# Differential attention woven into reordered key, value and query slots, its bias rows made in the glu slots, and its norm sums by plain fp32 matmuls

## The reference, cut to what matters

```python
def shared_kv(x, kv_norm, kv_w, k_norm):
    kv = rms_norm(x, kv_norm) @ kv_w
    nk = 2 * N_HEADS * HEAD_DIM
    k = rms_norm(kv[..., :nk].reshape(bsz, seqlen, N_HEADS, 2, HEAD_DIM), k_norm)
    v = kv[..., nk:].reshape(bsz, seqlen, N_HEADS, 2 * HEAD_DIM)
...
def diff_attention(h, k, v, rel_bias, w_q, q_norm, ...):
    q = rms_norm((h @ w_q).reshape(bsz, seqlen, N_HEADS, 2, HEAD_DIM), q_norm)
    ...
        bias = rel_bias[t5_causal_bucket(rel)].astype(f32).transpose(2, 0, 1)
        s = jnp.einsum("bqhcd,bkhcd->bhcqk", qc, k).astype(f32) * scale
        s = s + bias[None, :, None]
        s = jnp.where(rel <= 0, s, NEG_INF)
        pm = jax.nn.softmax(s, axis=-1)
        attn = pm[:, :, 0] - lam * pm[:, :, 1]
        return jnp.einsum("bhqk,bkhe->bqhe", attn.astype(v.dtype), v)
    ...
    o = rms_norm(o, subln) * (1.0 - lam_init)
    return o.reshape(bsz, seqlen, N_HEADS * 2 * HEAD_DIM) @ w_o
```

## Time and profile before

| What | Value |
|---|---|
| Median of 3 runs | 1396.17 us (1394.51 to 1400.16) |
| The profiled execution | 1395.5 us |
| Its span, first to last instruction | 1393.6 us |
| PE busy in the span | 1321.2 us (95%) |
| POOL, ACT, DVE busy | 1017.5, 687.4, 683.8 us |
| Mean granted PE clock | 0.974 |

### The profile page before, as it was taken

How to read it: one execution, slowest core, us unless ns; L and a number is a source line. 1 busy time by engine, 2 the same in 40 slices (tenths; PEclk the granted TensorE clock), 3 DMA queues, 4 the chain that set the end, 5 groups by cost and what they waited for, 6 DMA issues and landing times.

```text
span 1393.6 us, 27925 instructions
## 1 busy us (share of the span) xinstructions
PE 1321.2 (95%) x11024; PEld 1265.1 (91%) x11024; DVE 683.8 (49%) x1175; ACT 687.4 (49%) x960; POOL 1017.5 (73%) x794
## 2 busy tenths in 40 slices
PE   6989999999999689999999959999999999999999
PEld 6879999999989469999998837999999998899999
DVE  8994555556545866555565694211113454311112
ACT  7716544444656676444456445544445444644442
POOL 1227988888778418888878672888887765888885
PEclk9999999999999799999999968999999999999999
DMA  6314555555456305555554430555554432455540
GB/s 256 122 62 152 189 182 182 181 181 181 152 138 244 121 1 190 182 181 181 181 181 152 153 121 31 182 182 181 181 181 164 177 118 95 152 182 182 182 149 30
DMA packets 33879, 217.07 MB, mean 156 GB/s; under 512 B 3683, under 2 KB 7428, under 8 KB 8196
## 3 DMA queue, kind: packets, MB, share of 16 engines
q1 hardware_dynamic: 30096, 211.14, 42.9%
q10 hardware_dynamic: 3700, 4.75, 1.4%
HBM read 213.26 MB, written 2.62 MB: 155 GB/s over the span
## 4 chain that ended last, share of the span: by engine, by line
PE 78%; DVE 12%; ACT 5%; issue 3%; POOL 1%; DMA 1%; DVEq 0%; ACTq 0%; SPq 0%; POOLq 0%
PE up L1349 18%; PE up L1350 17%; PE up L1351 17%; PE acc L1349 6%; PE acc L1351 6%; PE acc L1350 6%; ACT w_hi L417 2%; PE up L1469 1%; DVE opnd L795 1%; DVE mix L1117 1%; DVE mix L1235 1%; DVE mix L804 1%; DVE s_work L935 1%; DVE mix L1132 1%; DVE mix L1131 1%
## 5 line engine op out<-in xcount | busy, mean ns | idle before, releaser
L340 POOL TENSOR_TENSOR w_lo<-ring,w_hi 128x512 fp32r<-128x512 f32 x764 | 985.0, 1322 | 291.8 <-ACT w_hi L417 282.0
L1349 PE MATMUL up<-opnd,w_hi 128*128 128x256 f32 x2208 | 631.8, 286 | 8.7 <-POOL w_lo L340 2.2
L1350 PE MATMUL up<-opnd,w_lo 128*128 128x256 f32 x2208 | 625.3, 283 | 0.0
L1351 PE MATMUL up<-opnd,w_hi 128*128 128x256 f32 x2208 | 625.2, 283 | 0.0
L417 ACT ACTIVATE w_hi<-ring 128x2048 fp32r<-128x2048 f32 x193 | 368.3, 1910 | 267.5 <-PE up L1351 213.8
L1349 PEld LDWEIGHTS up<-opnd,w_hi 128*128 128x128 f32 x2208 | 424.0, 192 | 19.8 <-issue 10.9
L1350 PEld LDWEIGHTS up<-opnd,w_lo 128*128 128x128 f32 x2208 | 424.2, 192 | 0.4
L1351 PEld LDWEIGHTS up<-opnd,w_hi 128*128 128x128 f32 x2208 | 424.1, 192 | 0.0
L1349 PE MATMUL acc<-opnd,w_hi 128*128 128x256 f32 x736 | 208.5, 283 | 2.5 <-DVE opnd L1033 2.5
L1350 PE MATMUL acc<-opnd,w_lo 128*128 128x256 f32 x736 | 208.3, 283 | 0.0
L1351 PE MATMUL acc<-opnd,w_hi 128*128 128x256 f32 x736 | 208.3, 283 | 0.0
(11 more groups left out here) (238 smaller groups left out, 1358.9 us busy)
## 6 DMA issues: line engine op xcount, KB each, us to landing
ring<-in_stream SPq DMA_DIRECT2D x197, 1024.0 KB, 4.8
bias_rows<-mix ACTq DMA_DIRECT2D x1, 1536.0 KB
mix<-in_s_b SPq DMA_DIRECT2D x1, 1024.0 KB, 6.5
x<-in_x SPq DMA_DIRECT2D x1, 1024.0 KB, 8.5
mix<-in_s_c SPq DMA_DIRECT2D x1, 1024.0 KB, 12.5
mix<-bias_rows ACTq DMA_DIRECT2D x1, 1024.0 KB, 5.1
out_x<-x SPq DMA_DIRECT2D x8, 128.0 KB, 1.7
mix<-in_p ACTq DMA_DIRECT2D x2, 256.0 KB, 3.4
```

Of the source, the lines that this page charges most:

```text
L340: ins = nc.gpsimd.tensor_tensor(w_lo[:, b, cols], ring[:, r, cols], w_hi[:, b, cols].bitcast(f32), ALU.subtract)
L1349: MM(o, l_hi, r_hi, start=start, stop=False, skip_group_check=True)
L1350: MM(o, l_lo, r_hi, start=False, stop=False, skip_group_check=True)
L1351: return MM(o, l_hi, r_lo, start=False, stop=stop, skip_group_check=True)
```

## The change

- The 12 slots of `kvq` are taken in the order q0 q1 k0 v0 k1 q2 k2 v1 q3 k3 v2 v3, and the queries' operand is made before the keys'. SP's list of slots is written out for this stage.
- Attention runs between half-slots: `DIFF_AT` says after which half the scores of a head run, `DIFF_PV` the same for its values, `DIFF_OUT` for its output. The first two slots of `wo` are spread over the last half-slots by a table, as for the stick stage.
- Both query blocks of a head are one step now: four score matmuls, three transposes into one bank, one ACT copy, and values with 256 and 128 columns.
- Squares of the head norms are summed by one plain fp32 matmul of 512 columns; the rounded copy, DVE's remainder and `d_half_r` are gone.
- The one-hot load, the bias matmul and its copy move to glu slots 1, 4 and 5. ACT issues the 1.5 MB write right after the last glu slot, and the read back before ple0.

```diff
-UNITS = ["s5", "ffn0", "ple0", "kv", "q", "diff", "ffn1", "ple1", "even", "mixed", "ffn2",
+UNITS = ["s5", "ffn0", "ple0", "q", "kv", "diff", "ffn1", "ple1", "even", "mixed", "ffn2",
...
+DIFF_ORDER = ["q0", "q1", "k0", "v0", "k1", "q2", "k2", "v1", "q3", "k3", "v2", "v3"]
+DIFF_AT = [8, 10, 12, 14, 16, 18, 22, 24]
+DIFF_PV = [12, 14, 16, 18, 22, 23, 26, 28]
+DIFF_OUT = [19, 20, 20, 21, 25, 26, 29, 31]
+DIFF_HALVES = 32
...
@@ scalar engine, glu loop and after it
+                if m == 1:
+                    act.dma_start(d_oh, a["bias_oh"]).then_inc(dma["bias_oh"], 16)
...
+            c.wait("bias_sb")
+            act.dma_start(a["scratch"], d_row.unsqueeze(1).broadcast_to([HEADS, P, 384])).then_inc(dma["bias_w"], 16)
...
             act.dma_start(f_pe[:, 0:2], a["p0"]).then_inc(dma["pe0"], 16)
             pe_operand(0)
             ffn(0, "ple0")
-            ple(0, ["kv", "q"])
+            act.wait_ge(dma["bias_w"], 16)
+            act.dma_start(d_bias, a["scratch_toeplitz"]).then_inc(dma["bias_r"], 16)
+            ple(0, ["q", "kv"])
...
@@ vector engine, glu loop
+                if m == 5:
+                    c.wait("bias_ps")
+                    c.up_and_wait(V.tensor_copy(d_row, aux[0][0:HEADS, 0:384]), "bias_sb")
...
@@ tensor engine
+                if m == 4:
+                    pe.wait_ge(dma["bias_oh"], 16)
+                    c.up(MM(aux[0][0:HEADS, 0:384], d_oh[:, 384:384 + HEADS], d_oh[:, 0:384], start=True, stop=True),
+                         "bias_ps")
...
+            def diff_stats(n):
+                c.wait("hn_sq")
+                ...
+                c.up(MM(acc[:, 3], d_half, d_sq[:, n % 2], start=True, stop=True, skip_group_check=True), "hn_ssq")
...
+            fill = {24: [(0, range(4))], 25: [(1, range(4))], 26: [(0, [4]), (1, [4])], 27: [(0, [5]), (1, [5])],
+                    30: [(0, [6]), (1, [6])], 31: [(0, [7]), (1, [7])]}
+            for t in range(DIFF_HALVES):
+                i, half = t // 2, t % 2
+                if i < 12:
+                    if half == 0:
+                        o = begin_slot(S + i)
+                    diff_half(i, half, o)
+                for h in heads_at(DIFF_AT, t):
+                    diff_scores(h)
+                for g, ks in fill.get(t, []):
+                    if ks[0] == 0:
+                        banks[g] = begin_slot(wo + g)
+                    slot_part("diff", wo + g, banks[g], ks, fresh=(g == 0))
+                for h in heads_at(DIFF_PV, t):
+                    diff_values(h)
+                for h in heads_at(DIFF_PV, t - 1):
                     c.wait("o_sq")
                     c.up(MM(aux[h % 2][:, T:2 * T], ones, d_q[:, h], start=True, stop=True), "o_ssq")
+                for n in stats_at(t):
+                    diff_stats(n)
+                for h in heads_at(DIFF_AT, t - 2):
+                    diff_transposes(h)
```

More of the change, by code:

```diff
@@ L315, in listed @@
                     load(s % RING, slice(streamed(s), streamed(s) + 1))
[L317 to L321, removed]
+            done = RING
+            for name in ("kvq", "qkv"):
+                first = START[name] // RING * RING
+                steady(done, (first - done) // RING)
+                done = first + 3 * RING
+                listed(first, done)
+            steady(done, (N_SLOTS - done) // RING)
             listed(N_SLOTS // RING * RING, N_SLOTS)
@@ L688, in _, with diff_square, diff_root @@
[L688 to L692, removed]
+            def diff_square(n):
+                if n >= 2:
+                    act.wait_ge(sem("qk_ready"), n - 1)
+                c.wait("hn_raw")
+                c.up(A(d_sq[:, n % 2], d_tmp[:, n % 3], ACT.Square), "hn_sq")
+            def diff_root(n):
+                c.wait("hn_ssq")
+                b = d_sq[:, n % 2]
+                c.up_and_wait(A(b, acc[:, 3], ACT.Ln, scale=1.0 / HD, bias=eps), "hn_ln")
+                c.up(A(b, b, ACT.Exp, scale=-0.5), "hn_rstd")
@@ L1141, in _ @@
             ffn(0, "ple0")
-            ple(0, ["kv", "q"])
+            ple(0, ["q", "kv"])
             S, u0 = START["kvq"], BANK["kvq"]
[L1146 to L1152, removed]
-            c.wait("rstd")
+            c.wait("rstd")
@@ L1155, in diff_normed, with diff_projection @@
+            def diff_projection(i):
+                kind, g, u = DIFF_ORDER[i][0], int(DIFF_ORDER[i][1]), (u0 + i) % 2
+                if kind == "v":
+                    if g == 0:
+                        c.wait("rstd_tok")
+                    values(S + i, u, d_v[:, :, g * 256:(g + 1) * 256], 256)
+                    c.tell("up_free")
+                    c.tell("diff_v")
+                else:
+                    head_raw(DIFF_NORMED.index(i), S + i, u, d_tmp)
             def diff_normed(n):
+                name = DIFF_ORDER[DIFF_NORMED[n]]
+                g = int(name[1])
@@ L1161, in diff_normed, with diff_logits @@
                                                      ALU.mult, ALU.mult), "qk_ready")
[L1163 to L1181, removed]
+            def diff_logits(h):
+                c.wait("diff_scores")
+                for qb in range(2):
+                    nk = P * (qb + 1)
+                    L = d_l[:, qb].rearrange("p (c k) -> p c k", c=2)[:, :, 0:nk]
+                    bias = d_bias[:, h, 0:T] if qb else d_bias[:, h, P:T]
+                    c.up_and_wait(V.scalar_tensor_tensor(L, acc[:, 0:2, P * qb:P * qb + nk], HD ** -0.5,
+                                                         bias.unsqueeze(1).broadcast_to([P, 2, nk]), ALU.mult, ALU.add),
+                                  "diff_read")
+                    c.up(V.tensor_reduce(d_st[:, 40 + 2 * qb:42 + 2 * qb], L, AX.X, ALU.max, negate=True), "diff_max")
@@ new lines, in diff_probs @@
+            def diff_probs(h):
+                if h:
+                    c.wait("diff_at_ps")
+                for qb in range(2):
+                    nk = P * (qb + 1)
+                    L = d_l[:, qb].rearrange("p (c k) -> p c k", c=2)[:, :, 0:nk]
+                    c.wait("diff_exps", 2)
+                    r = d_st[:, 48 + 2 * qb:50 + 2 * qb]
+                    step(V.reciprocal(r, d_st[:, 44 + 2 * qb:46 + 2 * qb]))
+                    step(V.tensor_scalar(L[:, 1], L[:, 1], r[:, 1:2], neg_lam, ALU.mult, ALU.mult))
+                    c.up(V.scalar_tensor_tensor(d_a[:, qb, 0:nk], L[:, 0], r[:, 0:1], L[:, 1], ALU.mult, ALU.add),
+                         "diff_probs")
+                dve.wait_ge(sem("diff_probs"), c.of("diff_probs").value())
@@ new lines, in _ @@
+            for t in range(2, DIFF_HALVES):
+                if t % 2 == 0 and t <= 24:
+                    diff_projection(t // 2 - 1)
+                for n in stats_at(t - 2):
+                    diff_normed(n)
+                for h in heads_at(DIFF_AT, t - 1):
+                    if h == 0:
+                        dve.wait_ge(dma["bias_r"], 16)
+                    diff_logits(h)
+                for h in heads_at(DIFF_AT, t - 2):
+                    diff_probs(h)
+                for h in heads_at(DIFF_PV, t - 3):
@@ L1663, in _ @@
             assert used[0] == BANK["kvq"]
[L1664 to L1692, removed]
+            def diff_half(i, half, o):
+                b, kind = (S + i) % SPLIT, DIFF_ORDER[i][0]
+                name = "q" if kind == "q" else "kv"
+                if DIFF_ORDER[i] == "k0" and half == 0:
+                    c.wait("hi_ready", KT)
+                    c.wait("lo_ready", KT)
+                for k in range(4 * half, 4 * half + 4):
+                    if i == 0:
+                        c.wait("hi_ready")
+                        c.wait("lo_ready")
+                    for m in range(2):
+                        first, last = k == 0 and m == 0, k == KT - 1
+                        if kind == "v":
+                            w, q = slice(2 * k * P, (2 * k + 2) * P), slice(m * P, (m + 1) * P)
+                            ins = three(o[:, m], hi(name)[:, k, q], lo(name)[:, k, q], w_hi[:, b, w], w_lo[:, b, w],
+                                        first, last)
+                        else:
+                            w = slice((2 * k + m) * P, (2 * k + m + 1) * P)
+                            ins = three(o[:, m], w_hi[:, b, w], w_lo[:, b, w], hi(name)[:, k], lo(name)[:, k],
+                                        first, last)
+                    between(k, i == 1, 4 if i == 1 else 0)
+                if half:
+                    c.up(ins, "mm_done")
+                if i == 0:
+                    square_sums(half)
@@ L1696, in diff_values @@
                 if h >= 2:
                     pe.wait_ge(sem("o_ln"), h - 1)
[L1698 to L1715, removed]
-                    h = n // 2 - 4
+                o, v, at = aux[h % 2], d_v[:, :, h * P:(h + 1) * P], d_at[:, h % 2]
@@ L1727, in _ @@
+                for h in heads_at(DIFF_AT, t - 2):
+                    diff_transposes(h)
+            c.wait("hn_ln")
+            for g in range(2, 4):
```

(1 more changed line is left out.)

127 lines of the change are left out of this document (78 added, 49 removed).

## The result

The kernel after takes 1419.0 us (median of four runs, 1416.22 to 1420.67) where the kernel before took 1395.34 in the same comparison: a ratio of 1.0161, with a 95% interval of 1.0131 to 1.019. It is slower by 1.6%; I had forecast 1411 us and a range of 1396 to 1421. The median lies inside that range, but 1 us above the narrower 1401 to 1418 that I had given to the forecast's own case. The profiled execution took 1416.22 us, with a span of 1414.4 and a mean granted clock of 0.968, so the span grew by 20.8 us.

A forecast was written before the change was run, and what follows sets the result against it. PE was taken as the bound, a train of slots outside a few stretches. 1395.5 - 16.5 (attention) + 0.75 (bias matmul) + 29 (p0 wait) + 2 (half clock) = 1410.75, forecast as 1411 us, range 1396 to 1421.

The forecast's parts named there:

- the forecast's own case: Start of ffn0: p0 waits behind the whole bias write; 1411 us for the kernel, range 1401 to 1418, chance 0.65.
- The wait for p0: Start of ffn0: p0 queues behind the bias write on ACT's queue; PE waits 29 us (24 to 33).
- only half: Start of ffn0, rival: p0 waits for only about half of the write, 15 us; 1397 us, no change; chance 0.10.
- Not held up: Start of ffn0, rival: p0's packets run between the write's, attention saving stands alone; 1380 us; chance 0.13.
- The attention stretch: Second slot of kvq to end of wo: 118.2 us against 134.7, 16.5 us saved (11 to 24).
- heads, norm sums, breaks: Attention between half-slots: PE's fp32 work per head, its norm sum and two breaks, 3.7 us each, 29.6 for 8.
- `w_lo` and the clock: End of wo: rounding of its fourth slot comes late and PE waits; 4 us (0 to 6).
- slips of DVE: Attention between half-slots: most outputs fall behind halves 20 and 23, where DVE slips; 2 us (0 to 8).
- tail of the last head: End of attention: last head's chain, about 12 us, against 11 us of matmuls beside it; 2 us (0 to 5).
- The tie: Attention slots with a head: DVE needs 9.6 us a slot where PE needs 9.5.
- DVE bound: Attention, rival: DVE becomes the bound between half-slots, some 8 us of saving left; 1419 us; chance 0.12.
- The bias matmul: Glu: the moved matmul returns in PE's train of slots there and adds 0.75 us.

The follow-up runs named there:

- p0 first: The changed kernel with two DMA issues swapped, ACT issuing the load of p0 ahead of the 1.5 MB bias write; 1383.6 us, ratio 0.9917.
- half of the write first: The changed kernel with the bias write cut in two, 64 of 128 copies of each row ahead of p0 and 64 behind; 1404.78 us.
- the four quarters: The changed kernel with p0 loaded from POOL's queue and ACT issuing the write in four DMAs of 32 copies a row; 1398.33 us.
- the control: The changed kernel with p0 loaded from POOL's queue and ACT issuing the write only once p0 has landed; 1388.01 us.

## Why the prediction was right, and where its sizes were off

**The wait for p0** was right in mechanism and close in size. Forecast: p0 behind the whole write, 29 us of standing still (24 to 33) and 2 us of half clock. Measured: 30.4 us on PE, 30.05 more on ACT (33.0 - 2.95), and 2 us. The full length of the write stood ahead of the half of p0 that came last, as the forecast had it for the engines that both use; the other half passed at 165 to 168, which shortens nothing, since ACT needs both.

**The rival "only half"** failed for this change, though its picture of a dense first 17 us is real in this trace. Something like it came about where p0 goes on another queue: there half of p0 waits for just that dense part. "Not held up" is refuted where p0 is issued behind the write; its time of 1380 us is near what p0 first gives (1383.6).

**The attention stretch** was forecast at 118.2 us from the second slot of `kvq`. From the same point (397.1 + 34.85 = 431.95) to 553.43 it is 121.5 us, a saving of 13.2 and not 16.5. Windows of after over it:

```profile
431.95:463.69 31.74, 31.74 (x244) 28.71 (x243) 14.75 (x29) 20.44 (x34) 26.25 (x20) 1.00 0.42 144
463.69:499.00 35.31, 35.31 (x267) 31.54 (x266) 22.37 (x48) 25.56 (x66) 20.84 (x16) 1.00 0.35 126
499.00:512.00 13.00, 9.36 (x69) 7.78 (x68) 10.50 (x16) 7.07 (x9) 9.34 (x7) 1.00 0.33 122
...
536.50:553.43 16.93, 14.31 (x105) 13.93 (x104) 8.89 (x13) 9.86 (x15) 12.97 (x10) 0.90 0.25 74
```

| Term | Forecast, us | Measured, us |
|---|---|---|
| 14 slots of the stream | 80.6 | 80.6 |
| heads, norm sums, breaks | 29.6 | 28.6 (PE busy 110.9, less 80.6 and 1.7 of half clock) |
| `w_lo` and the clock | 4 | 3.9 (2.23 of wait, and 0.10 x 16.93 = 1.7 of clock) |
| slips of DVE | 2 | 3.6 |
| tail of the last head | 2 | 4.3 |
| other idle time | - | 0.4 |
| sum | 118.2 | 121.4 |

The period of a head is 9.07 us with a norm sum where I had 9.5: this is PE's timeline after, two heads running.

```profile
463.69 0.93 PE L1789 MATMUL acc<-mix 64*128 64x128 f32 x8
464.55 0.70 PE L1811 MATMUL side<-mix 128*128 128x256 f32 x2
465.09 0.38 PE L1812 MATMUL side<-mix 128*128 128x128 f32 x2
465.31 1.02 PE L1779 MATMUL acc<-mix 128*128 128x512 f32 x2
466.17 0.49 PE L1799 MATMUL acc<-par,mix 128*128 128x128 f32 x3
...
472.76 0.93 PE L1789 MATMUL acc<-mix 64*128 64x128 f32 x8
```

Scores 0.86, values 0.76, norm sum 0.86, transposes and sum of squares the rest: 3.31 on top of 5.76, and nothing for breaks in this period. The step that failed is DVE's 2 us for slips. The tie (9.6 against 9.5) was rightly seen, but I spread it. It falls in one place, between 499 and 512, where outputs of heads, output norms and the scores of head 6 meet; PE's waits there, timeline of after:

```profile
501.64 0.55 PE L1799 MATMUL acc<-par,mix 128*128 128x128 f32 x3 [1.02 <-DVE mix L1244]
...
510.24 0.93 PE L1789 MATMUL acc<-mix 64*128 64x128 f32 x8 [2.29 <-DVE mix L1216]
```

DVE itself is slowed there: the two-input instruction of L1216 takes 0.75 us with POOL idle (at 498.82) and 1.70 beside it (at 508.48), 0.95 more, where the earlier trace rows had given 0.75. The second size that was off is the tail: PE waits for DVE's and ACT's operands five times behind the last head, 1.37 + 0.90 + 0.90 + 0.57 + 0.60 = 4.3 us, where my range went to 5. "DVE bound" as a rival (8 us of saving left) did not come about. Its price of 1419 us is the measured median to the microsecond, but by chance: the saving is 13.2 us, and the time alone wouldn't have told this rival from the forecast.

**Glu.** The bias matmul was priced at 0.75 us; the profiled execution of the kernel after comes out of glu 3.0 us later. Two marks of ACT, its table load at the start of glu and its last copy there, split this: 41.62 us before (111.40 to 153.02) and 44.03 after (112.00 to 156.03), with 0.6 us lost ahead of glu. Of the eleven kernels with the new glu slots eight take 42.55 us between the marks, and three 44.03: after, p0 first and half of the write first. So the moved matmul and what goes with it cost 0.93 us, and the other 1.48 are a fall of the clock that some executions show and others don't. The window of after, to be read beside a clock of 1.00 and 28 matmuls in the same window before, and the issue of the one-hot matrix:

```profile
113.00:116.00 3.00, 3.00 (x17) 3.00 (x16) 1.01 (x3) 1.67 (x5) 3.00 (x3) 0.51 0.79 320
```

```profile
120.55 0.57 ACTq L584 DMA_DIRECT2D mix<-in_bias_oh  x1
```

The load is issued behind the dip, so it doesn't set it off; what does stays open.

**The sum.** In its terms: 1395.5 - 13.2 + 3.0 + 30.05 + 2 = 1417.35, less 0.8 us elsewhere, against 1416.22 measured. Of the 5.5 us by which the profiled execution is above the 1410.75 of the sum, 3.3 are the saving, 2.3 glu (0.2 the matmul, the rest this execution's own), 1 the wait, and other places gave back 1. This execution was the fastest of the four; the median lies 2.8 us above it.

## What to carry to other kernels

Before a large DMA is moved, look at what the same engine issues behind it: the write from 8 partitions takes some 20 us a MB here, and a load that follows it on that queue is whole only when all of the write is through, so the small load that an engine needs at once goes first. (No run writes the same bytes from more partitions, so that the 8 partitions are what makes it slow is not shown.) Two DMAs in another order turn 1.6% lost into 0.8% won. A stage that is woven between slots gains until two of its parts meet on the second engine; find that place in the waits and move one of them by a slot, and see that a rounding at the border isn't queued behind work that waits for the stage's end.

## What the runs showed of the hardware

- Another queue is only half an escape from such a write. PE's wait falls from 30.4 to 19.7 us, where the other order leaves 0.35. Half of a 256 KB load passes at once, the other half stands for about 17 us, until some 550 packets of the write are through, whether the write is one DMA or four. The Trainium skill (DMA: Bandwidth & Descriptors, "Queues, rings and completion order") says that an engine goes from one queue to the next only after a whole packet of descriptors, with 9 to 17 as a typical number and 64 at most. If the write runs on 8 engines, the typical number doesn't fit these traces (8 x 17 = 136 packets, an estimate, against 550), and the highest does (8 x 64 = 512). Against it stand the four quarters, whose borders after 256 packets gave p0 no turn, and the control, where the write's high share lasts over 800 packets. No trace shows the borders of such packets, so this cause is not shown.
- The issue of a DMA can itself be held up. Behind the write the issue of p0 takes 7.50 us on ACT's sequencer, and behind two writes 29.77 us, where it takes 0.36 alone. Nothing was lost by it here, since ACT had to wait for p0 anyhow.
